# Two chained transformer blocks in fp32: the mixers' attention regrouped in pairs of items, and their norm factors moved between engines

## The reference

```python
for l in range(DEPTH):
    h = rms_norm(x, ffn1_norm[l])
    x = x + 0.5 * swiglu(h, ffn1_w_gate[l], ffn1_w_up[l], ffn1_w_down[l])
    h = rms_norm(x, mix_norm[l])
    (na_q, na_k, na_v, df_q, df_k, df_v, gq_q, gq_k, gq_v, dl_q, dl_k, dl_v) = split_in_proj(h @ w_in[l])
    ...
    o = jnp.concatenate([o_a, o_b, o_c, o_d], axis=-1)
    x = x + o @ w_out[l]
    h = rms_norm(x, ffn2_norm[l])
    x = x + 0.5 * swiglu(h, ffn2_w_gate[l], ffn2_w_up[l], ffn2_w_down[l])
```

```python
        p = jax.nn.softmax(s, axis=-1)
        a = p[0] - lam * p[1]
        return jnp.einsum('bhqk,bhkd->bhqd', a.astype(vt.dtype), vt)
    ...
    o = rms_norm(o, out_gain) * (1.0 - lambda_init)
```

## Time and profile before

| | us |
|---|---|
| median of 3 runs (lowest, highest) | 1925.69 (1920.82, 1929.4) |
| the profiled execution | 1924.7 |
| its span, first to last instruction | 1922.9 |
| PE, DVE, ACT, POOL busy | 1709.3, 1281.0, 916.9, 103.4 |
| mean granted clock of PE | 0.93 |

### The profile page before, as it was taken

How to read it: one execution, slowest core, us unless ns; L and a number is a source line. 1 busy time by engine, 2 the same in 40 slices (tenths; PEclk the granted TensorE clock), 3 DMA queues, 4 the chain that set the end, 5 groups by cost and what they waited for, 6 DMA issues and landing times.

```text
span 1922.9 us, 22440 instructions
## 1 busy us (share of the span) xinstructions
PE 1709.3 (89%) x7968; PEld 1403.2 (73%) x7968; DVE 1281.0 (67%) x2231; ACT 916.9 (48%) x1727; POOL 103.4 (5%) x141
## 2 busy tenths in 40 slices
PE   7999976799999999966699998967899987689998
PEld 5888755588887788755587887757788776677886
DVE  5786758777776777667867775575745556865553
ACT  6444534554445444534554445554643455645442
POOL 0000112000000000011100000011000000200000
PEclk9999987599999999997599999967999998689999
DMA  8876521157776777522147884302566542045551
GB/s 305 271 267 231 196 88 55 34 194 264 263 242 202 265 262 256 196 77 79 43 154 261 275 261 146 127 12 99 164 208 197 169 145 88 23 143 201 182 187 66
DMA packets 99678, 331.66 MB, mean 172 GB/s; under 512 B 18625, under 2 KB 18881, under 8 KB 99057
## 3 DMA queue, kind: packets, MB, share of 16 engines
q1 hardware_dynamic: 84928, 277.84, 43.6%
q10 hardware_dynamic: 14640, 52.39, 8.1%
HBM read 329.09 MB, written 1.10 MB: 172 GB/s over the span
## 4 chain that ended last, share of the span: by engine, by line
PE 71%; DVE 17%; ACT 7%; issue 3%; POOL 1%; DMA 1%; SPq 0%; ACTq 0%; POOLq 0%; DVEq 0%
PE PS L578 21%; PE PS L580 21%; PE PS L579 21%; DVE Wl L1316 4%; ACT Wh L970 2%; DVE QTl L1316 2%; PE PS L638 1%; DVE st L1454 1%; DVE WK L1451 1%; ACT WK L1060 1%; PE PS L718 1%; PE PS L699 1%; DVE PTl L1487 1%; DVE st L1456 1%; DVE GQ L1382 1%
## 5 line engine op out<-in xcount | busy, mean ns | idle before, releaser
L1316 DVE TENSOR_TENSOR Wl<-raw,Wh 128x1024 fp32r<-128x1024 f32 (+2 forms) x339 | 397.2, 1213 | 109.7 <-ACT Wh L970 109.0
L578 PE MATMUL PS<-Wh,Hh 128*128 128x512 f32 (+2 forms) x1028 | 409.4, 398 | 61.2 <-DVE Wl L1316 34.5
L579 PE MATMUL PS<-Wl,Hh 128*128 128x512 f32 (+2 forms) x1028 | 402.5, 392 | 0.0
L580 PE MATMUL PS<-Wh,Hl 128*128 128x512 f32 (+2 forms) x1028 | 402.2, 391 | 0.0
L970 ACT ACTIVATE Wh<-raw 128x1024 fp32r<-128x1024 f32 (+2 forms) x339 | 334.1, 1035 | 23.8 <-PE PS L580 13.2
L578 PEld LDWEIGHTS PS<-Wh,Hh 128*128 128x128 f32 x1028 | 197.8, 192 | 109.9 <-DVE Wl L1316 41.1
L580 PEld LDWEIGHTS PS<-Wh,Hl 128*128 128x128 f32 x1028 | 197.9, 192 | 39.8
L579 PEld LDWEIGHTS PS<-Wl,Hh 128*128 128x128 f32 x1028 | 198.3, 193 | 37.0
L1316 DVE TENSOR_TENSOR QTl<-raw,QTh 128x1024 fp32r<-128x1024 f32 x175 | 206.3, 1219 | 18.8 <-ACT QTh L970 18.5
L578 PE MATMUL PS<-QTh,Hh 128*128 128x512 f32 x500 | 195.5, 391 | 1.0 <-DVE QTl L1316 0.9
L580 PE MATMUL PS<-QTh,Hl 128*128 128x512 f32 x500 | 194.8, 390 | 0.0
(11 more groups left out here) (208 smaller groups left out, 2418.4 us busy)
## 6 DMA issues: line engine op xcount, KB each, us to landing
raw<-in_ffn SPq DMA_DIRECT2D x396, 512.0 KB, 5.2
BT<-in_ada ACTq DMA_DIRECT2D x96, 512.0 KB, 4.4
raw<-in_win SPq DMA_DIRECT2D x64, 512.0 KB, 4.4
raw<-in_wo SPq DMA_DIRECT2D x32, 512.0 KB, 3.9
raw<-in_win SPq DMA_DIRECT2D x8, 420.0 KB, 4.1
BT<-in_nab SPq DMA_DIRECT2D x2, 1024.0 KB, 6.8
raw<-in_win SPq DMA_DIRECT2D x8, 256.0 KB, 2.8
BT<-in_t5b SPq DMA_DIRECT2D x2, 1024.0 KB, 4.9
```

The source lines that it names most:

```text
L578: e.matmul(out_, xh, wh, start=start, stop=False)
L579: e.matmul(out_, xh, wl, start=False, stop=False)
L580: return e.matmul(out_, xl, wh, start=False, stop=stop)
L1316: e.tensor_tensor(low(p)[:, 0:w], raw[p % RAW][:, 0:w], high(p)[:, 0:w].bitcast(f32), ALU.subtract).then_inc(w_lo, 1)
```

## The change

**Pairs of items.** Attention goes in pairs: four heads, or both parts of two diff heads, and one tile of queries; 10 pairs in a mixer "a" and 8 in "b". A pair has events S (scores, DVE bias and maximum), E (exponentials), N (division), T (transposes, split) and V (values, copies out), which `walk` places one by one. DVE's instructions take a whole pair (1024 columns) where they took an item (512). Scores have one set of four banks, so the scores of a pair wait for the exponentials of the one before. The first head's division goes from GpSimd to ACT (a copy with a scale).

**Norm factors.** The power -0.5 of each group's sums goes from DVE's Newton steps to one GpSimd instruction (L1851 of the new kernel). The gain of columns that aren't rotated, and the factor of the scores, are put in the scale of the split after the transpose (`q_scale`); the gain of rotated columns goes into tables of cosine and sine times gain, which GpSimd computes once a mixer (`tables`). GpSimd's pass over q and k is gone, and DVE rotates both tiles at once. Columns of the projection are reordered on the host so that the two rotated-together halves stand together.

**One pair per projection step.** The projection's second step is now dilated q and k, and each further step and tile has one pair beside it. The last four pairs lie between chunks of tile 0's output projection, which accumulates in banks 0 and 7.

**Head norm per tile.** Diff outputs are squared, summed and normed per tile; GpSimd writes the power -0.5 of four sums directly over 4x64 columns (L1852), operands read with a step of 0. PE's "rows" of a tile wait for it (`o_rs`).

Core of the diff:

```diff
+        def step(p, *then):
+
+            return [("S", p, 0, 0), *([("T", p - 1, 0, 0)] if p else []), ("E", p, 0, 0), *then, ("N", p, 0, 0)]
+
+        def wo(t, *chunks):
+            return [("wo", (c,), t, 0) for c in chunks]
+
         ev += [("proj", 0, 0, 0), *mid, ("proj", 1, 0, 0), ("proj", 0, 1, 0), ("norm", 0, 0, 0), ("proj", 1, 1, 0), ("rope", 0, 0, 0),
-               ("proj", 2, 0, 0), ("turn_qk", 0, 0, 0), ("att", -1, 0, 0), ("proj", 2, 1, 0), ("att", 0, 0, 0),
-               ("proj", 3, 0, 0), ("norm", 1, 0, 0), ("att", 1, 0, 0), ("proj", 3, 1, 0), ("rope", 1, 0, 0), ("att", 2, 0, 0),
-               ("proj", 4, 0, 0), ("turn_qk", 1, 0, 0), ("att", 3, 0, 0), ("norm", 2, 0, 0), ("proj", 4, 1, 0), ("att", 4, 0, 0),
-               ("rope", 2, 0, 0), ("att", 5, 0, 0), ("proj", 5, 0, 0), ("turn_qk", 2, 0, 0), ("att", 6, 0, 0), ("norm", 3, 0, 0),
-               ("att", 7, 0, 0), ("proj", 5, 1, 0), ("att", 8, 0, 0), ("rope", 3, 0, 0), ("att", 9, 0, 0), ("turn_qk", 3, 0, 0),
-               *(("att", i, 0, 0) for i in range(10, ITEMS["a"] + 3)), ("mix", 0, 0, 0),
-               ("wo", (0,), 0, 0), ("wo", (0,), 1, 0), ("sums", 0, 0, 0), ("wo", (1,), 0, 0), ("wo", (1,), 1, 0),
-               ("wo", (2,), 0, 0), ("wo", (2,), 1, 0), ("rows", 0, 0, 0), ("wo", (3,), 0, 0), ("wo", (3,), 1, 0),
-               ("wo", (4,), 0, 0), ("wo", (4,), 1, 0), ("wo", (5, 6, 7), 0, 0), *end[0], *scale[0],
-               ("wo", (5, 6), 1, 0), nxt[0], ("wo", (7,), 1, 0), nxt[1]]
+               ("turn_qk", 0, 0, 0), ("proj", 2, 0, 0), ("norm", 1, 0, 0),
+               *step(0, ("rope", 1, 0, 0)), ("proj", 2, 1, 0),
+               *step(1, ("turn_qk", 1, 0, 0)), ("proj", 3, 0, 0), ("V", 0, 0, 0),
+               *step(2), ("proj", 3, 1, 0), ("V", 1, 0, 0), ("norm", 2, 0, 0),
...
+               ("V", 5, 0, 0), ("S", 6, 0, 0), ("chunks", 0, 0, 0), ("E", 6, 0, 0), ("N", 6, 0, 0), ("chunks", 1, 0, 0),
+               *wo(0, 0, 1), *step(7), *wo(0, 2), ("V", 6, 0, 0),
+               *step(8), *wo(0, 3), ("V", 7, 0, 0),
+               *step(9), *wo(0, 4), ("sums", 0, 0, 0), ("V", 8, 0, 0), ("T", 9, 0, 0), *wo(0, 5), ("rows", 0, 0, 0), ("V", 9, 0, 0),
+               ("wo", (6, 7), 0, 0), ("sums", 1, 0, 0), *end[0], *scale[0], *wo(1, 0, 1, 2), ("rows", 1, 0, 0),
+               *wo(1, 3), nxt[0], *wo(1, 4, 5), nxt[1], ("wo", (6, 7), 1, 0)]
...
+            def diff_rows(stage, t):
+                l = stage[1]
+                e.wait_ge(o_rs, 2 * l + t + 1)
+                if t == 0:
+                    e.wait_ge(s_oa, pair0[stage] + 9)
+                    e.wait_ge(s_od, pair0[stage] + 9)
...
+                for n in range(4):
+                    i, k = n // 2, n % 2
+                    ins = e.activation(s[:, i, k, 0:nk], src[:, i, k, 0:nk], ACT.Exp, bias=st[:, NM + 4 * (p % 2) + n:NM + 4 * (p % 2) + n + 1],
+                                       accum_out=st[:, Z + 4 * p + n:Z + 4 * p + n + 1])
...
+                for i in range(2):
+                    o = ZR + 4 * p + 2 * i + k
+                    ins = e.activation(s[:, i, k, :], s[:, i, k, :], ACT.Copy, scale=st[:, o:o + 1])
+                ins.then_inc(s_p0, 1)
...
+                    if p >= 2:
+                        e.wait_ge(s_turn, turned(stage, p - 2))
+                    dst = SB[:, p % 2, :, :, 0:nk]
+                    e.tensor_tensor(dst, src, it["bias"], it["op"]).then_inc(s_bias, 1)
+                    e.wait_ge(s_bias, bias_no(stage, p))
+                    src = dst
+                e.tensor_reduce(nm, src, AX.X, ALU.max, negate=True).then_inc(s_max, 1)
...
+                if not it["diff"]:
+                    ins.then_inc(s_rec, 1)
+                    e.wait_ge(s_rec, gp + 1)
+                    e.tensor_tensor(s[:, :, 1, 0:nk], s[:, :, 1, 0:nk], zr[:, :, 1:2].to_broadcast([128, 2, nk]),
+                                    ALU.mult).then_inc(s_p1, 1)
...
+                e.wait_ge(g_sq, 8 * l + 2 * x + 2)
+                e.tensor_reduce(st[:, SS:SS + 2 * nh], NW[:, 0:2 * nh * n].rearrange("p (h n) -> p h n", n=n),
+                                AX.X, ALU.add).then_inc(g_sum, 1)
...
+                e.wait_ge(g_rs, 4 * l + x + 1)
+                q = A[:, :, c0:c0 + nh * n].rearrange("p t (h n) -> p t h n", n=n)
+                rs = st[:, RS:RS + 2 * nh].rearrange("p (t h) -> p t h", t=2)
+                e.tensor_tensor(q, q, rs.unsqueeze(3).to_broadcast([128, 2, nh, n]), ALU.mult).then_inc(g_scaled, 1)
...
-            def diff_root(l):
-                e.wait_ge(o_sum, l + 1)
-                own.mark(e.tensor_copy(st[:, SS:SS + 8], PS[:, 4, 0:8]))
-                own.mark(root(0, 8, 64, mul=1.0 - lam_init(l)))
-                own.after()
-                e.tensor_copy(WK[:, 1024:1536].rearrange("p (g n) -> p g n", n=64),
-                              st[:, RS:RS + 8].unsqueeze(2).to_broadcast([128, 8, 64])).then_inc(o_rs, 1)
...
-            def root(a, b, n):
-
-                s, r = st[:, SS + a:SS + b], st[:, RS + a:RS + b]
-                own.mark(e.tensor_scalar(s, s, 1.0 / n, EPS, ALU.mult, ALU.add))
+            def root(a, b, n, mul=1.0, to=None):
+
+                s, r, m = st[:, SS + a:SS + b], st[:, RS + a:RS + b], mhalf[:, 0:b - a]
+                own.mark(e.tensor_scalar(s, s, 1.0 / n / mul ** 2, EPS / mul ** 2, ALU.mult, ALU.add))
                 own.after()
-                return e.tensor_tensor(r, s, mhalf[:, 0:b - a], ALU.pow)
+                if to is None:
+                    return e.tensor_tensor(r, s, m, ALU.pow)
+                return e.tensor_tensor(to, s.unsqueeze(2).to_broadcast(to.shape), m.unsqueeze(2).to_broadcast(to.shape), ALU.pow)
+
+            def tables(l):
+
+                e.wait_ge(gq_in, 16 * (l + 1))
+                if l == 0:
+                    e.wait_ge(ct_in, 16)
+                else:
+                    e.wait_ge(g_rope, 3 * l)
+                for g, name in ((1, "dl"), (2, "ax"), (3, "df")):
+                    w = TAB[g][1]
+                    h = w // 2
+                    gains = GQ[:, ROWS[g]:ROWS[g] + 2 * w].rearrange("p (k n) -> p k n", k=2)
+                    for t in range(2):
+                        c, sn = (cn(name + x, t * w, t * w + w).unsqueeze(1).to_broadcast([128, 2, w]) for x in "cs")
+                        e.tensor_tensor(table(g, 0)[:, t, :, :], c, gains, ALU.mult)
+                        e.tensor_tensor(table(g, 1)[:, t, :, 0:h], sn[..., 0:h], gains[..., h:w], ALU.mult)
+                        ins = e.tensor_tensor(table(g, 1)[:, t, :, h:w], sn[..., h:w], gains[..., 0:h], ALU.mult)
+                ins.then_inc(g_tab, 1)
...
-            def probs(stage, i):
-                its = items_of[stage]
-                it, gi = its[i], item0[stage] + i
-                if it["part"] != "pair":
-                    return
-                e.wait_ge(s_rec, gi + 1)
-                p0 = SB[:, i % 3, 0, 0:it["nk"]]
-                e.tensor_scalar(p0, p0, st[:, ZR + 2 * i:ZR + 2 * i + 1], None, ALU.mult).then_inc(s_p0, 1)
...
+                    if what == "norm":
+                        e.wait_ge(g_sum, 4 * k + x + 1)
+                        root(0, 2 * GROUPS[x][1], GROUPS[x][2]).then_inc(g_rs, 1)
                         if x == 0:
-                            e.wait_ge(gq_in, 16 * (k + 1))
-                        for t in range(2):
-                            e.wait_ge(g_scaled, 8 * k + 2 * x + t + 1)
-                            q = A[:, t, c0:c0 + nh * n]
-                            e.tensor_tensor(q, q, GQ[:, c0:c0 + nh * n], ALU.mult).then_inc(g_gain, 1)
-                    elif what == "att" and 0 <= x - 1 < ITEMS[kind]:
-                        probs(stage, x - 1)
+                            tables(k)
+                    elif what == "sums":
+                        e.wait_ge(o_get, 2 * k + x + 1)
+                        lam_init = 0.8 - 0.6 * math.exp(-0.3 * k)
+                        root(40 + 4 * x, 44 + 4 * x, 64, 1.0 - lam_init,
+                             diff_sq(x).rearrange("p c (h n) -> p (c h) n", h=2)).then_inc(o_rs, 1)
```

848 lines of the change are left out of this document (427 added, 421 removed).

## The result

| | before | after |
|---|---|---|
| median of the runs, us | 1924.49 (1920.82 to 1929.4, 4 runs) | 2042.61 (2035.37 to 2050.14, 4 runs) |
| ratio, 95% interval | | 1.0612 [1.0567, 1.0658] |
| the profiled execution, its span | 1924.7, 1922.9 | 2041.77, 2040.0 |
| PE, DVE, ACT, POOL busy | 1709.3, 1281.0, 916.9, 103.4 | 1699.2, 1221.1, 940.6, 232.8 |

The change made the kernel 118 us slower. I had predicted 2003 us with a range up to 2040: the direction was right, the size was 40 us short, and the measured time lies just above the range. It is near what my third rival gave (2047 us: the power at its full price, the mixers gaining about 20 us instead of 42).

The account below looks back on a forecast made before the run. With PE 89% busy, 113 of a first-block mixer's 195 us were put to attention, norms and waits, nearly every chain passing through DVE. 2 x (-42 + 81) = +78 on 1924.7 gave 2003 us, range 1850 to 2040.

Parts of the forecast that it names:

- third rival: First-block mixers: power costs 39.6 us, gain 20 instead of 42 as pairs wait on score banks and DVE; 2047 us, chance 0.07.
- The wide power: Head norm in first-block mixers: GpSimd's 256-column power takes 39.6 us, mostly exposed; with PE's slow restart +81 us a mixer.
- rivals 1 and 2: Head-norm power cheaper with width, 10.8 us, 1875 us in all, chance 0.22; or cheap as plain arithmetic, 1.3, 1841, 0.15.
- The contention: DVE splits beside GpSimd's wide power slow down, 2.1 us more each time; the sum would be 8 us higher.
- The gain of 42 us a first-block mixer: Without the head norm's cost, front and back stretch gain 21 us each: -42 us a mixer, 15 either way.
- DVE sets the step, 11.4 us of it each: Front stretch: each projection step asks 11.4 us of DVE, 8.7 of PE; 105 us instead of 126.3.
- The q and k norm powers at nothing: First-block q and k norms: powers of 2.2 to 5.3 us covered by DVE's other work, charged nothing; uncovered, 3 us a mixer.
- The late pairs and the tail, 43.4 us: Back stretch: four pairs at 5.5 us, 22 in all, then output projection and rest; 43.4 us instead of 68.5.
- ACT takes over the division, covered: First-block mixers: 20 copies of 256 columns, at most 10 us on ACT, covered while PE has a projection step beside.
- Second-block mixers 0, 5 either way: Second-block mixers: pairs of 128 keys gain about what pairs of 256 keys lose; charged 0, 5 us either way.

Follow-up runs that it names:

- narrow_power: The changed kernel with the head norm's power taken of 4 columns, then copied over 4x64 by GpSimd: 1892.16 us, ratio to before 0.9831.
- light_splits: narrow_power with DVE splitting only 128 of each weight piece's up to 1024 columns in the first-block mixers: 1884.39 us.
- no_rotation: narrow_power without the rotation of q and k in the first-block mixers: 1875.41 us.
- short_qk_powers: narrow_power with the four q and k norm powers of a first-block mixer taken of one column each: 1873.47 us.
- late_pairs2: narrow_power with the last four first-block pairs reordered, next scores and maximum ahead of the division, values one pair later: 1889.66 us.
- narrow_gpsdiv: narrow_power with the division of one head of two moved from ACT back to GpSimd, all 36 pairs: 1905.16 us.

## Why the prediction was wrong, step by step

**The wide power: right.** 39.6 us predicted from the difference between one and two columns, 41.1 measured; exposure and restart 81 us a mixer predicted, 77.0 and 77.8 measured. The rivals 1 and 2 (10.8 and 1.3 us) fell. The contention that the prediction weighed for the wide power, 2.1 us for the splits beside each, didn't come. Four of DVE's splits lie beside the second one (407.83 to 448.95), and they take what they take alone; of these the first three:

```profile
410.82 1.23 DVE L1375 TENSOR_TENSOR Wl<-raw,Wh 128x1024 fp32r<-128x1024 f32 x1 [2.17 <-ACT Wh L1024]
411.97 2.35 DVE L1375 TENSOR_TENSOR QTl<-raw,QTh 128x1024 fp32r<-128x1024 f32 x2
```

The Trainium skill, page "GPSIMD Engine Reference", section 3.1 "Elementwise — side-by-side cycle accounting", gives about 2.6 cycles an element, which it ties to the two inputs of a `tensor_tensor` and measures on an addition; an estimate from it is near 1 us for 256 columns. The power is such a `tensor_tensor`, and this trace has 0.159 us a column for it and 41.1 us in all, against 0.40 us for a copy of 256 columns. The measurement decides: the page's figure doesn't hold for a power.

**The gain of 42 us a first-block mixer if the head norm cost nothing: this is the step that failed.** narrow_power measures it directly: 22.2 and 25.1 us. In the profiled runs: 84 - 47.3 = 36.7 us of gain that didn't come, 162 - 154.8 = 7.2 us less for the powers, 6.1 more in the second-block mixers and 3.5 in the feed-forward stages make 39.1 of the 38.8 us between 2003 and 2041.8. Held against narrow_power's first mixer, half of it is missing in front (115.9 us against 105) and half in the back (56.7 against 47.4, which is 43.4 and the four counted in front). What the runs showed in its place is 22 to 25 us: the front stretch goes by the chain of norm, power and rotation and by what stands behind it in DVE's order, and not by DVE's total. In it:

- *DVE sets the step, 11.4 us of it each.* Its total was right (115 predicted, 115.2 measured), its role wrong. The sum had 25 us of start and 80 for the six pairs with their gaps; in narrow_power the first scores come after 31.4 us, 3.3 of them a wait for the first group's scaling, and the pairs take 84.4. So more is missing in the start, which five projection steps of 5.4 us fill by themselves, than in the pairs. Scores of pairs 2 and 3, and of 4 and 5, stand 8.8 us apart, with PE at work throughout; those of 1 and 2, and of 3 and 4, where a group of q and k comes in between, 17.4 and 16.9. light_splits and no_rotation show that DVE's time on the chain counts and its other time hardly does.
- *The q and k norm powers at nothing, 3 us if the cover is gone.* 7 us a mixer (short_qk_powers). I had bounded their duration well (5.3 us predicted for 32 columns, 5.4 measured) and hid it beside DVE's other work, without asking which instruction of DVE stands behind the rotation in its order and who waits for that.
- *The late pairs and the tail, 43.4 us.* From the scores of pair 6 to the sums of tile 0 it took 27.8 us and not 22, with a wait of 4.7 us of PE for the first remainder of the mixed chunks; the rest took 28.9 and not 21.4 and 4. Overlapping the pairs didn't change it (late_pairs2), so for this half the cause isn't shown by an experiment and stays open; the profile names the 4.7 us, 3.1 for ACT's squares, and a granted clock of 0.81 in the 27.8 us and 0.89 in the rest.

**ACT takes over the division, covered:** right as far as narrow_gpsdiv shows (4 us a mixer slower on GpSimd).

**Second-block mixers 0, 5 either way:** -0.4 and +6.5 us in the changed kernel, +6.9 and +9.2 in narrow_power with the same second block. The attention was charged nothing and lost 4.1 and 2.9 us; the rest is PE's clock behind it, which the bound didn't allow for.

**The range.** Rival 3 had the size of the gain (20 us) and a chance of 0.07; it gave it partly to DVE's 11.4 us a step, which light_splits refutes. Its evidence was in the rows: DVE was busy 89.7 of 126.3 us in front, so PE's waits for it were waits for its place in the order and not for a full engine. A range that ended at 2040 left out most of it.

## What to carry to other kernels

Price an operation by its own rows at two sizes, however small: 1 and 2 columns gave a 256-column power to 4%. Compute a factor once at its narrowest and broadcast it with a copy; here one line is worth 150 us. When work leaves an engine that is idle more than a quarter of the time, count it only where it stands on the chain that something waits for, and for each instruction with a long input ask what stands behind it in its engine's order.

## What the runs showed of the hardware

- A GpSimd power (fp32, exponent -0.5, the only one that was run) is linear in the columns of its output, also where its operands are read with a step of 0: 0.55 us at 1 column, 1.01 at 4, 2.91 at 16, 5.43 at 32, 41.1 at 256, 82.9 at 512; a copy of 256 columns takes 0.40 us there.
- Runs of one kernel differ by up to 16 us, and differences of medians don't add up. The unchanged second block took 346.1 to 358.4 us in ten profiles; behind its attentions PE's granted clock came back between 0.3 and 6.4 us after the first matmul of the output projection. Whether that accounts for all of the spread stays open, since the other runs of each kernel have no profile.
- Beside a GpSimd power whose operands are read with a step of 0, DVE's 128x1024 splits ran at their usual 1.2 us; beside GpSimd's 128x512 multiplications two of them had taken 4.49 us instead of 2.35.
- Ten small transposes ahead of each wait raised the mean granted clock from 0.935 to 0.957, in the second block's attentions from 0.65 to 0.82 or more, and the attentions got no shorter than in other kernels without them.
